# Attention heads of one stage in pairs of row halves, with one part of them as a single batch, on Trainium2

## What is computed

```python
# NSA: three attentions of the same queries, each weighted by a gate of its head
s_c = einsum('bqkgd,bnkd->bkgqn', qb, kc) * scale          # kc: 15 compressed keys
p_c = masked_softmax(s_c, cmp_end[None, :] <= t[:, None])
o_c = einsum('bkgqn,bnkd->bqkgd', p_c, vc)
...                                                        # o_s: selected blocks, o_w: window
o = gb[..., 0:1] * o_c + gb[..., 1:2] * o_s + gb[..., 2:3] * o_w
# MoBA
p = masked_softmax(concatenate([s_sel, s_own]), concatenate([m_sel, m_own]))
```

## Time and profile before

| | before |
|---|---|
| median of 3 runs | 2846.85 us |
| profiled execution, span from first to last instruction | 2845.0 us |
| TensorE matmul busy | 2729.3 us (96%) |
| VectorE busy | 1994.5 us (70%) |
| ScalarE busy | 1346.1 us (47%) |
| GpSimd busy | 301.1 us (11%) |
| attention part of the stage (first filler to last store) | 2091.99 to 2179.05 us |

### The profile page before, as it was taken

One profiled execution on the slowest core, in us unless ns is written; L12 is line 12 of the kernel. 1 busy time (PEld: TensorE's weight loads), 2 busy tenths in 40 slices (PEclk: granted clock), 3 DMA queues, 4 the chain that ended last, 5 costly groups with the idle time before them and its releaser, 6 DMA issues.

```text
span 2845.0 us, 43721 instructions
## 1 busy us (share of the span) xinstructions
PE 2729.3 (96%) x17208; PEld 2398.6 (84%) x17208; DVE 1994.5 (70%) x3872; ACT 1346.1 (47%) x2201; POOL 301.1 (11%) x162
## 2 busy tenths in 40 slices
PE   7999999999999999999999999999999899898997
PEld 7879999998888897899999988887867678786776
DVE  5668988975555655689889655556667669656588
ACT  4433544444455434345444444554334357453475
POOL 0006930000000001069200000000100000000000
PEclk9999999999999999999999999999899999999999
DMA  6354554455655552445544556555521369522486
GB/s 222 103 175 134 178 164 156 160 170 187 194 193 192 192 188 94 165 134 177 164 157 156 172 189 194 192 193 182 137 78 25 131 221 353 170 88 77 166 298 227
DMA packets 175420, 480.08 MB, mean 169 GB/s; under 512 B 27232, under 2 KB 43504, under 8 KB 175216
## 3 DMA queue, kind: packets, MB, share of 16 engines
q1 hardware_dynamic: 172112, 474.34, 50.6%
q10 hardware_dynamic: 3104, 2.95, 0.3%
HBM read 475.65 MB, written 1.57 MB: 168 GB/s over the span
## 4 chain that ended last, share of the span: by engine, by line
PE 88%; DVE 6%; ACT 2%; POOL 2%; issue 1%; DMA 0%; ACTq 0%; SPq 0%; DVEq 0%; POOLq 0%
PE ps L134 86%; POOL ring_rest L154 2%; PE ps L137 2%; DVE big L162 1%; DVE spl L154 1%; DVE st L178 1%; ACT big L140 1%; DVE xb L162 1%; ACT whi L140 1%; DVE st L162 0%; DVE big L154 0%; ACT spl L140 0%; POOL big L154 0%; DVE grouped L154 0%; DVE xr L154 0%
## 5 line engine op out<-in xcount | busy, mean ns | idle before, releaser
L140 ACT ACTIVATE whi<-ring 128x1024 fp32r<-128x1024 f32 x512 | 542.6, 1060 | 686.1 <-PE ps L134 684.3
L134 PE MATMUL ps<-xr,whi 128*128 128x256 f32 x4096 | 749.8, 285 | 11.1 <-POOL ring_rest L154 10.7
L154 DVE TENSOR_TENSOR ring_rest<-ring,whi 128x1024 fp32r<-128x1024 f32 x412 | 503.6, 1223 | 317.9 <-ACT whi L140 317.9
L134 PEld LDWEIGHTS ps<-xr,whi 128*128 128x128 f32 x4096 | 639.7, 192 | 14.0 <-DVE big L184 8.6
L134 PE MATMUL ps<-whi,Ar 128*128 128x512 f32 x2048 | 631.3, 389 | 4.5 <-DVE Ar L154 4.5
L134 PE MATMUL ps<-xr,ring_rest 128*128 128x256 f32 x2048 | 580.5, 283 | 0.0
L154 DVE TENSOR_TENSOR spl<-ring,spl 128x1024 fp32r<-128x1024 f32 (+3 forms) x384 | 435.9, 1163 | 116.6 <-ACT spl L140 107.9
L134 PEld LDWEIGHTS ps<-whi,Ar 128*128 128x128 f32 x2048 | 384.4, 188 | 85.0 <-DVE Ar L154 5.0
L140 ACT ACTIVATE spl<-ring 128x1024 fp32r<-128x1024 f32 (+3 forms) x384 | 373.9, 1008 | 97.9 <-PE ps L134 77.9
L134 PE MATMUL ps<-ring_rest,Ar 128*128 128x512 f32 x1024 | 398.4, 389 | 0.0
L134 PEld LDWEIGHTS ps<-xr,ring_rest 128*128 128x128 f32 x2048 | 394.1, 192 | 0.0
(11 more groups left out here) (129 smaller groups left out, 2463.7 us busy)
## 6 DMA issues: line engine op xcount, KB each, us to landing
ring<-in_peer_u_dram SPq DMA_DIRECT2D x256, 512.0 KB, 3.5
ring<-in_peer_v_dram SPq DMA_DIRECT2D x256, 512.0 KB, 3.5
ring<-in_moe_gate_up_dram SPq DMA_DIRECT2D x128, 512.0 KB, 5.0
ring<-in_moe_w_down_dram SPq DMA_DIRECT2D x64, 512.0 KB, 5.3
ring<-in_peer_w_q_dram SPq DMA_DIRECT2D x32, 512.0 KB, 5.0
ring<-in_sb_w_in_dram SPq DMA_DIRECT2D x24, 512.0 KB, 4.6
ring<-in_ab_w_in_dram SPq DMA_DIRECT2D x20, 512.0 KB, 5.6
ring<-in_w_out_dram SPq DMA_DIRECT2D x16, 512.0 KB, 4.5
```

Source lines behind the costliest of these rows:

```text
L134: return self.e.matmul(o, l, r, start=start, stop=stop)
L140: return self.e.activation(o, i, f, **k)
L154: return self.e.tensor_tensor(o, a, b, op)
```

## The change

The 64 jobs become 24 **pairs**: both row halves of one head and branch, in one step. TensorE's scores of a pair go side by side into one bank (128 and 256 keys); three transposes go into one bank, and one copy of 128x384 moves them; three output matmuls fill 128 columns of one bank, and one VectorE instruction stores both halves. The scores are scaled by -0.125 and the mask (0 or -1e30, still added) is taken with a running **minimum** (`add_min`), so that the accumulated value can be the bias of the exponential (scale -1) at once; the negation is gone. One copy in three is VectorE's, the others ScalarE's. The NSA pairs are stored in a buffer of their own, and **GpSimd** adds them to `mix`.

The compressed branch is a **batch** of all 8 heads: `cmp_scores_pe` (16 matmuls of 15 columns after step 10), mask, maximum, centring, one exponential, one sum and factors for all, four transposes after step 11 (`cmp_turn_pe`), and in the attention part four matmuls of 256 columns (`cmp_out_pe`). The values stand block-diagonally (`vcC`, with the new constant `block4`), four copies of `hidv` make the rows. `compressed_pe` writes into banks 2 and 3 instead of 4 to 7. Fillers: 3 in each of the first 3 steps, none after. Core of the diff:

```diff
         def compressed_pe(pe):
...
             for k in range(2):
-                take(pe, 4 + k)
-                pe.matmul(bank(4 + k)[:, 0:15], w2pad[:, k, :], hidg[:, 0, k, :], True, True).then_inc(*psum.next(("kc", k)))
-                give(pe, 4 + k, (vec, ("kc", k)))
-                take(pe, 6 + k)
-                pe.matmul(bank(6 + k)[0:15, 0:64], hidg[:, 1, k, :], cw2[:, 1, :], True, True).then_inc(*psum.next(("vc", k)))
-                give(pe, 6 + k, (vec, ("vc", k)))
+                take(pe, 2 + k)
+                pe.matmul(bank(2 + k)[:, 0:15], w2pad[:, k, :], hidg[:, k, :], True, True)
+                pe.matmul(bank(2 + k)[:, 64:128], hidv[:, k, :, :].rearrange("p r n -> p (r n)"), cw2[:, 1, :], True, True).then_inc(
+                    *psum.next(("compressed", k)))
+                give(pe, 2 + k, (vec, ("kc", k)), (vec, ("vc", k)))
...
+                  9: [lambda e: turns_pe(e, ("qM", 0), ("qM", 1)), compressed_pe], 10: [lambda e: cmp_scores_pe(e)],
+                  11: [lambda e: turns_pe(e, ("kM", 0), ("kM", 1)), lambda e: cmp_turn_pe(e)]},
...
+        def pair_pe(pe, s):
+            i = s
+            if i < NP:
+                j, b = pairs[i], score_bank(i)
+                take(pe, b)
+                for t in range(2):
+                    ins = pe.matmul(bank(b)[:, KEYS[t][0]:KEYS[t][1]], j["q"][:, 128 * t:128 * t + 128], j["k"][:, 0:128 * t + 128],
+                                    True, True)
+                ins.then_inc(*psum.next(("pair_scores", i)))
+                give(pe, b, (vec, ("pair_max", i)))
+            i = s - 2
+            if 0 <= i < NP:
+                b = 2 + i % 2
+                take(pe, b)
+                pe.wait_ge(*acted.at(("pair_exp", i)))
+                for k in range(3):
+                    ins = tp(pe, bank(b)[:, 128 * k:128 * k + 128], pair_p(i)[:, 128 * k:128 * k + 128])
...
+            i = s - 3
+            if 0 <= i < NP:
+                j, b, PT = pairs[i], 4 + i % 2, pair_pt(i)
+                take(pe, b)
+                pe.wait_ge(*copied(i).at(("pair_copied", i)))
+                v = [pr[:, k, j["v"]:j["v"] + 64] for k in range(2)]
+                pe.matmul(bank(b)[:, 0:64], PT[:, 0:128], v[0], True, True)
+                pe.matmul(bank(b)[:, 64:128], PT[:, 128:256], v[0], True, False)
+                pe.matmul(bank(b)[:, 64:128], PT[:, 256:384], v[1], False, True).then_inc(*psum.next(("pair_out", i)))
...
+        def pair_dve(dve, s):
+            i = s - 4
+            if 0 <= i < NP:
...
+                if j["gate"] is not None and i >= 4:
+                    dve.wait_ge(*gps.at(("pair_added", i - 4)))
+                dve.tensor_tensor(held, bank(4 + i % 2)[:, 0:128].rearrange("p (t e) -> p t e", t=2),
+                                  f.unsqueeze(2).to_broadcast([128, 2, 64]), ALU.mult).then_inc(*vec.next(("pair_stored", i)))
+            i = s
+            if i < NP:
...
+                for t in range(2):
+                    d = slice(*KEYS[t])
+                    dve.add_min(pair_s(i)[:, d], bank(b)[:, d], (C("causal"), caus1)[t], -0.125,
+                                pair_stat(i, 0)[:, t:t + 1]).then_inc(*vec.next(("pair_max", i, t), ("pair_max", i)))
+            i = s - 1
+            if 0 <= i < NP:
+                j = pairs[i]
+                dve.wait_ge(*acted.at(("pair_exp", i)))
+                dve.reciprocal(pair_stat(i, 2), pair_stat(i, 1)).then_inc(*vec.next(("pair_factor", i)))
+                if j["gate"] is not None:
...
+                    dve.tensor_tensor(pair_stat(i, 2), pair_stat(i, 2), j["gate"], ALU.mult).then_inc(*vec.next(("pair_factor", i)))
+            i = s - 2
+            if 0 <= i < NP and copied(i) is vec:
...
+                dve.tensor_copy(pair_pt(i), bank(2 + i % 2)[:, 0:384]).then_inc(*vec.next(("pair_copied", i)))
...
+        def pair_act(act, s):
+            i = s - 1
...
+                    act.activation(pair_p(i)[:, d], pair_s(i)[:, d], ACT.Exp, bias=pair_stat(i, 0)[:, t:t + 1], scale=-1.0,
+                                   accum_out=pair_stat(i, 1)[:, t:t + 1]).then_inc(*acted.next(("pair_exp", i)))
...
         def nsa_pe(pe):
...
             busy(pe, 4)
             join(pe, "N")
-            heads_pe(pe, "nsa", jobsN, planN, PTN, PmN)
+            for s in range(NP + 3):
+                if s == 1:
+                    cmp_out_pe(pe)
+                busy(pe, 3 if s < 3 else 0)
+                pair_pe(pe, s)
```

More of the change, by code:

```diff
@@ new lines, in cmp_turn_pe, with cmp_turn_act @@
+        def cmp_turn_pe(pe):
+            take(pe, 6)
+            pe.wait_ge(*acted.at("cmp_exp"))
+            flat = scr[:, 7584:8096]
+            for k in range(4):
+                ins = tp(pe, bank(6)[:, 128 * k:128 * k + 128], flat[:, 128 * k:128 * k + 128])
+            ins.then_inc(*psum.next("cmp_turned"))
+            give(pe, 6, (acted, "cmp_copied"))
+        def cmp_turn_act(act):
+            act.wait_ge(*psum.at("cmp_turned"))
+            act.activation(cmpPT, bank(6), ACT.Copy).then_inc(*acted.next("cmp_copied"))
@@ new lines, in cmp_out_pe @@
+        def cmp_out_pe(pe):
+            pe.wait_ge(*acted.at("cmp_copied"))
+            for k in range(2):
+                pe.wait_ge(*vec.at(("vc", k)))
+            for t in range(2):
+                take(pe, 4 + t)
+                for k in range(2):
+                    ins = pe.matmul(bank(4 + t)[:, 256 * k:256 * k + 256], cmpPT[:, 256 * t + 128 * k:256 * t + 128 * k + 128],
+                                    vcC[:, k, :], True, True)
+                ins.then_inc(*psum.next(("cmp_out", t)))
+                give(pe, 4 + t, (vec, ("cmp_stored", t)))
@@ new lines, in cmp_store_dve @@
+        def cmp_store_dve(dve):
+            dve.wait_ge(*vec.at("cmp_factors"))
+            for t in range(2):
+                dve.wait_ge(*psum.at(("cmp_out", t)))
+                dve.tensor_tensor(mix[:, t, 0:512].rearrange("p (h e) -> p h e", h=8), bank(4 + t).rearrange("p (h e) -> p h e", h=8),
+                                  cmpF[:, t, :].unsqueeze(2).to_broadcast([128, 8, 64]), ALU.mult).then_inc(
+                                      *vec.next(("cmp_stored", t)))
+        pairs = []
@@ new lines, in pair_pool @@
+        def pair_pool(pool):
+            for t in range(2):
+                pool.wait_ge(*vec.at(("cmp_stored", t)))
+            for i, j in enumerate(pairs):
+                if j["gate"] is None:
+                    continue
+                o = mix[:, :, j["col"]:j["col"] + 64]
+                pool.wait_ge(*vec.at(("pair_stored", i)))
+                if i % 2:
+                    pool.wait_ge(*gps.at(("pair_added", i - 1)))
+                pool.tensor_tensor(o, o, pair_held(i), ALU.add).then_inc(*gps.next(("pair_added", i)))
@@ L2098, in nsa_act @@
             join(act, "N")
[L2099 removed]
+            for s in range(NP + 3):
+                pair_act(act, s)
             acted.close(("end", "nsa"))
```

161 lines of the change are left out of this document (119 added, 42 removed).

## The result

The changed kernel takes **2807.1 us** (median of 4 runs, 2805.7 to 2808.2) against 2847.0 for the kernel before on the same chip (4 runs, 2840.5 to 2847.5): ratio 0.9865, 95% interval 0.9849 to 0.9881. The profiled executions differ by as much: spans of 2806.0 and 2845.0. Where the 39 us lie is read in five places.

The account below looks back on a forecast made before the run. TensorE was taken to bound the attention part. Its -28.2 us and the projection part's -1.4 sum to -29.6, from the span of 2845.0 to 2815.4; with 1.85 for the median, 2817 us, range 2809 to 2830.

Parts of the forecast that it names:

- a pace by VectorE at 2.6 us: Rival: VectorE or the round trip paces the pairs at 2.6 us, giving 9.6 back: 2827 us; chance 0.15.
- serial rounds: Rival: late output copies hold up later scores on TensorE, a pair at 3.4 us, about 2846 us; chance 0.05.
- The pair, 2.20 us: TensorE's time per pair in the attention part: 1.05 + 0.68 + 0.43 + 0.04 = 2.20 us; 24 pairs, 52.8 us.
- The scores: Term of the pair on TensorE: 0.42 (128 keys) + 0.63 (256 keys) = 1.05 us.
- lower bound of 2.13: Lower bound for a pair: the earlier MoBA head less its two fillers, 2.59 - 2 x 0.23 = 2.13 us.
- The rule on weight loads: Skill's rule, set aside: loads overlap matmuls only where row groups differ; by it about 9 us longer, 2826 us.
- The small terms: Attention part besides the pairs: compressed outputs 1.8, 13 fillers 3.0, `join` 0.5, drain 0.8 us.
- The projection part, -1.4: Part ahead of attention: idle -3.1, clock -2.6, compression matmuls -0.6, small scores +4.5, transposes +0.4: -1.4 us.
- I take no fall: Projection part: no clock fall with the new small scores; a fall would give about 3.4 us back.
- More gain by falls elsewhere: Rival: clock falls in later stages shift away with the new timing as well, 2808 us; chance 0.08.
- Low clock without fillers: Rival: without fillers TensorE is held at 1.2 GHz through the attention part, 58 us more, 2875 us; chance 0.05.
- The memory heads: Heads without fillers, two transposes in 1.44 us, at clock 1.00 through 12 us; cited against the rival of 1.2 GHz.

Follow-up runs that it names:

- experiment 3: Changed kernel with one filler in each step from the fourth on: 2810.3 us.
- Experiment 1: Changed kernel with each pair's 256-key scores moved behind its transposes: 2820.0 us; the same with three fillers in each of the first five steps: 2817.3 us.
- experiment 2: Changed kernel with two pairs' scores in one block every second step: 2806.3 us; the same with three fillers in each of the first five steps: 2806.0 us.
- Experiment 10: Kernel before with only the compression's results moved to banks 2 and 3, without the small scores: 2841.0 us.
- experiments 5 and 6: Kernel before without attention-part fillers from step 6 on: 2882.0 us; kernel before with fillers up to step 29 and none from step 30: 2871.7 us.
- experiment 7: Changed kernel without the nine fillers of its first three steps: 2845.1 us.
- experiment 8: Changed kernel with running maximum, its negation by two small VectorE instructions a pair, and exponential at scale 1: 2848.1 us.
- experiment 9: Changed kernel with the negations back and three fillers in each of the first five steps: 2814.0 us.
- the first run of experiment 2: Changed kernel with two pairs' scores in one block every second step, without the six added fillers: 2806.3 us.

## Why the forecast was right in kind and short in size

- **The bound.** TensorE set the attention part before and sets it after; the rivals of a pace by VectorE at 2.6 us and of serial rounds are out, since VectorE waits for scores in each pair.
- **The pair, 2.20 us: this step failed.** It is 1.94, outside its own bounds of 2.13 to 2.3, and 24 x 0.26 = 6.2 is what the attention part gained more. Of the terms, the output with its late start was 0.72 and is 0.71. The transposes with the change to 64-row scores were 0.43 and are 0.38. The scores were 1.05 and are 0.85 (experiment 3). In the earlier trace rows a score matmul of 0.42 or 0.63 is a block of 64-row matmuls by itself, entered from 128-row matmuls and left to them, so each number holds most of one entry and one exit, 0.20 us. I added the two and so counted this twice, though the pair has both scores in one block: 0.20 of the 0.26. (The rest of an entry, 0.09, stands in the piece ahead: six output passes take 0.62 with a filler behind them, experiment 3, and 0.71 with scores.) Experiment 1 puts the second block back and gets the 0.39, experiment 2 saves one in two NSA pairs and gets 0.34. My lower bound of 2.13, today's head less its fillers at 0.23 each, was no bound. It had the blocks still apart, and with them apart and no filler the pair is 2.33: a filler in the old head cost (2.59 - 2.33) / 2 = 0.13, not 0.23. It stood right behind the scores, where it may cover part of their exit; behind the outputs, in experiment 3, it cost 0.22.
- **The rule on weight loads.** In experiment 2 six output passes stand 0.61 apart from the next piece and three transposes behind them 0.34, 0.10 to 0.11 each, though every pass uses all rows; I read this as weight loads that are hidden behind the pass before. A price shows only between 64-row and 128-row matmuls. The Trainium skill (TensorE: Matmul & The Clock Gate, part 3) has loads overlap only where the row group differs, though in the same part it also lets a load into the background weight buffer go ahead. The first half does not fit these traces: passes on the same rows follow each other without a bare load (one that no running pass covers), and the price stands where the row count changes. That passes on different rows overlap does show: it is what two MoBA heads gain in experiment 2.
- **The small terms.** 13 fillers, `join` (0.27, and 0.18 ahead of the first outputs), compressed outputs and drain: 6.1 forecast, 6.0 measured.
- **The projection part, -1.4.** It is -0.6. The idle went, the scores were dear by 3.4, not 4.5. But "I take no fall" was wrong: f gained 0.6 and not 2.6. Experiment 10 shows the 2.2 that f gives without the small scores, so the fall came with them.
- **More gain by falls elsewhere** (0.08) came in part: some 4 us, in executions that differ from each other by as much. No run ties them to the change, and I count them as luck. Against the runs of the kernel before at 2841 the gain is 34 us, and without the 4 us the time would be some 2811, inside the range though not by the right pair.
- **Low clock without fillers** (0.05) was right in kind, too dear (58 us) and judged too lightly. The memory heads that I held against it keep 1.00 over their 12 us, while the single jobs of this stage lost it within some 4 us of their last filler (experiments 5 and 6): one stream does not speak for another, and what sets them apart no run shows. Experiments 7 and 8 show the new stream losing it from the start on, at 36 to 41 us. With its nine fillers in the first steps the changed kernel kept it in all eight executions, without them in none of ten. The Trainium skill (TensorE: Matmul & The Clock Gate, part 4) says that transposes are no work for the clock; a pair holds three of them in thirteen passes at either clock, so no run here tells what part they have in it.

| kernel | us | attention part's clock |
|---|---|---|
| changed | 2807.1 | held |
| changed, no start fillers | 2845.1 | lost |
| changed, negations back | 2848.1 | lost in 9 of 10 |
| the same, start filled | 2814.0 | held |
| scores apart | 2820.0 | lost in 2 of 10 |
| scores apart, start filled | 2817.3 | held |
| before, no fillers from step 6 | 2882.0 | lost |
| before, none from step 30 | 2871.7 | lost |

Open: why two of ten executions with the scores apart lost the clock and eight did not. The profiled one, which lost it, idled 0.24 us at the first outputs; the changed kernel idled 0.18, experiment 9 0.27 between fillers, and the first run of experiment 2 idled 0.41 (2108.47) with the same nine fillers, and all these kept it. So the length of that gap does not decide by itself. That it is the gap that loses the clock, in experiments 7 and 8, rests on experiment 8, whose fillers were the changed kernel's and whose first wait alone was longer; experiment 9 shortened it and added fillers at once, and no run shortened it alone. In experiment 7 the missing fillers are a rival to the gap of 1.13 us that comes with them.

## What to carry to other kernels

Price a matmul sequence by its changes: here matmuls that use the same rows followed each other with no price between them, so put those of 64 rows together, and where two of them lie in different halves of the rows, side by side. When a cost is read off a trace, ask what stands on both sides of it there. When fillers are taken out, look at the clock in every execution and at the start above all: a stream may keep the clock it has and not win it back, and here a bad start then cost some forty microseconds.

## What was not expected of the hardware

- One block more of 64-row matmuls in a stream of 128-row ones costs 0.39 us at 2.4 GHz, with the passes unchanged.
- Scores of two heads in different halves of the rows, one behind the other, ran at the same time: two such pairs took 2.91 us, two with both in the same half 3.55 (experiment 2).
- The same pairs ran at granted clock 1.00 for 40 us and at 0.50 for 68 us with no idle time between the pairs in either; which of the two was settled in the first steps. In no trace that lost it did it come back within the part.
- At 0.50 a pair took 3.58 us against 1.94, 1.84 times.
- 32 passes of 15 columns behind 24 passes of 512 went with a fall to about half clock, and a filler behind every eight did not prevent it.
